# A hybrid decoder trunk on one core: GpSimd's weight sums start behind another tile

## The reference

```python
for l in range(DEPTH):                       # DEPTH = 2
    h = rms_norm(x, g_mix[l])
    z = h @ w_in[l]
    qa, ka, va, ga, ub, vb, qc, kc, vc, gates = split_cols(z)
    ya = silu(ga) * (rms_normalize(retention(rotary(qa), rotary(ka), va)) * ret_norm_g[l])
    yb = spatial_gating(gelu(ub), gelu(vb), ...)
    # 3 groups of dilated attention, combined by their softmax denominators
    yc = sum(softmax(lses)[g] * outs[g] for g in range(3))
    merged = sum(sigmoid(gates)[:, :, b] * (y[b] @ w_branch[l, b]) for b in range(3))
    x = x + merged @ w_o[l]
    h = rms_norm(x, g_ffn[l])
    gate, up = jnp.split(h @ w_gate_up[l], 2, axis=-1)
    x = x + (silu(gate) * up) @ w_down[l]
```

## Time and profile before

| | us |
|---|---|
| median of 3 runs | 1905.05 |
| profiled execution | 1904.88 |
| span of the profiled execution | 1903.1 |
| TensorE busy | 1889.8 |
| VectorE busy | 1241.8 |
| ScalarE busy | 850.4 |
| GpSimd busy | 96.9 |

### The profile page before, as it was taken

One profiled execution on the slowest core, in us unless ns is written; L12 is line 12 of the kernel. 1 busy time (PEld: TensorE's weight loads), 2 busy tenths in 40 slices (PEclk: granted clock), 3 DMA queues, 4 the chain that ended last, 5 costly groups with the idle time before them and its releaser, 6 DMA issues. The chain is left out here.

```text
span 1903.1 us, 26512 instructions
## 1 busy us (share of the span) xinstructions
PE 1889.8 (99%) x10600; PEld 1696.9 (89%) x10600; DVE 1241.8 (65%) x1617; ACT 850.4 (45%) x1190; POOL 96.9 (5%) x148
## 2 busy tenths in 40 slices
PE   8999999999999999999999999999999999999999
PEld 7888888888888899899888888888888888998998
DVE  7767746666566786377577677566665667863775
ACT  5544444444334464155335444444443344642554
POOL 0000001111111000000000000011111110000000
PEclk9999999999999999999999999999999999999999
DMA  5322347777787455366333222577777774653663
GB/s 203 94 75 71 86 114 206 193 195 197 200 213 208 125 177 174 100 191 197 122 100 95 68 78 80 143 191 194 207 199 197 210 195 128 189 160 104 201 211 123
DMA packets 85897, 295.68 MB, mean 155 GB/s; under 512 B 20368, under 2 KB 20624, under 8 KB 84624
## 3 DMA queue, kind: packets, MB, share of 16 engines
q1 hardware_dynamic: 73104, 218.49, 37.0%
q0 software_dynamic: 12672, 75.51, 17.5%
HBM read 291.79 MB, written 77.66 MB: 194 GB/s over the span
## 5 line engine op out<-in xcount | busy, mean ns | idle before, releaser
L1076 ACT ACTIVATE w_high<-raw 128x1024 fp32r<-128x1024 f32 x396 | 418.3, 1057 | 780.1 <-PE bank L851 651.0
L1284 DVE TENSOR_TENSOR w_low<-raw,w_high 128x1024 fp32r<-128x1024 f32 x396 | 483.0, 1222 | 142.8 <-ACT w_high L1076 136.1
L851 PE MATMUL bank<-h_high,w_high 128*128 128x512 f32 x1344 | 518.7, 386 | 9.0 <-DVE h_low L1289 8.2
L851 PE MATMUL bank<-h_low,w_high 128*128 128x512 f32 x1344 | 510.1, 380 | 0.0
L851 PE MATMUL bank<-h_high,w_low 128*128 128x512 f32 x1344 | 510.1, 380 | 0.0
L851 PEld LDWEIGHTS bank<-h_high,w_high 128*128 128x128 f32 x1344 | 254.7, 190 | 45.3 <-issue 8.2
L851 PEld LDWEIGHTS bank<-h_high,w_low 128*128 128x128 f32 x1344 | 254.5, 189 | 36.2
L851 PEld LDWEIGHTS bank<-h_low,w_high 128*128 128x128 f32 x1344 | 254.7, 189 | 35.1
L851 PE MATMUL bank<-in_high,w_high 128*128 128x512 f32 x672 | 255.4, 380 | 0.0
L851 PE MATMUL bank<-in_low,w_high 128*128 128x512 f32 x672 | 254.7, 379 | 0.0
L851 PE MATMUL bank<-in_high,w_low 128*128 128x512 f32 x672 | 254.7, 379 | 0.0
(11 more groups left out here) (166 smaller groups left out, 2451.7 us busy)
## 6 DMA issues: line engine op xcount, KB each, us to landing
raw<-weights SPq DMA_DIRECT2D x325, 512.0 KB, 4.2
weight_sums<-weights POOLq DMA_DIRECT2D x108, 512.0 KB, 6.5
raw<-weight_sums SPq DMA_DIRECT2D x72, 512.0 KB, 4.1
weight_sums<-weight_sums POOLq DMA_DIRECT2D x36, 512.0 KB, 4.0
turned<-rows SPq DMA_DIRECT2D x3, 768.0 KB, 7.4
xT<-x_t SPq DMA_DIRECT2D x8, 256.0 KB, 5.7
decay_sb<-decay SPq DMA_DIRECT2D x8, 256.0 KB, 4.0
out_t<-xT SPq DMA_DIRECT2D x8, 256.0 KB, 4.5
```

The lines of the kernel that those rows point to most:

```text
L851: return pe.matmul(o, w, m, start=start, stop=stop)
L1076: act.activation(w_high[:, PART_SLOT[s], :, :], raw[:, s % RAW_SLOTS, :, :], ACT.Copy).then_inc(part_high_w.sem, 1)
L1284: dve.tensor_tensor(w_low[:, PART_SLOT[s], :, :], raw[:, s % RAW_SLOTS, :, :], w_high[:, PART_SLOT[s], :, :], ALU.subtract).then_inc(part_ ...
```

## The change

One argument of one wait in GpSimd's program. The first DMA of the sums of a layer waited until VectorE had evacuated `("rq", 0)`; it now waits until VectorE has evacuated `("k", 3, 0)` of the same layer, 13 tiles earlier. No instruction comes or goes, and the instructions of all five engines stand in the same order as before.

```diff
@@ -706,7 +706,7 @@
             for layer in range(DEPTH):
-                pool.wait_ge(tile_stored.sem, tile_stored.at(layer * STRIDE, AT["rq", 0]))
+                pool.wait_ge(tile_stored.sem, tile_stored.at(layer * STRIDE, AT["k", HEADS - 1, 0]))
                 for n, u in enumerate(QUICK_UNITS):
                     first = AT["quick", u, 0]
```

## The result

| | kernel before | changed kernel |
|---|---|---|
| median of 8 runs, us | 1905.56 (1904.66 to 1906.71) | 1914.14 (1909.56 to 1918.63) |
| ratio, 95% interval | | 1.0045 (1.0036 to 1.0055) |
| profiled execution, us | 1904.88 | 1914.38 |
| its span, us | 1903.1 | 1912.6 |

The change costs 8.6 us at the median, and the runs now spread over 9 us where they spread over 2. The forecast was 1907.3 us with a range to 1912.0: too low, and the measured median lies outside.

A forecast was written before the change was run, and what follows sets the result against it. TensorE's queue was taken as the bound from end to end. Profiled 1904.88 us, no gain, plus 2.3 us of swap delay (1.3 and 1.0) gave 1907.2, plus 0.17 to the median: 1907.3 us, range 1904.5 to 1912.0.

The forecast's parts named there:

- What bounds, and that the end of the sums gains nothing: TensorE's queue bounds from end to end; sums ending sooner gain at most 0.21 us per layer.
- Weight loads of head 3 cost 0: Loads beside the early sums: closest has 11.7 us until its split on ScalarE, slowest landed after 8.6; cost 0.
- The bound of 8.6 us: Slowest landing of a weight load beside the sums in the old trace, taken as worst; still leaves 3 us.
- The swap is the transfer: Softmax maxima and sums, written to DRAM and read back reordered; four swaps, heads 2 and 3, now lie beside the sums.
- the margins of 2.28, 2.16, 0.62 and 2.16 us: How late swaps may be before TensorE waits: heads 2 and 3 of layer 0, then of layer 1; sum 7.22 us.
- most of all at 1154: Largest new TensorE wait foreseen at 1154 us, head 2 of layer 1, where the margin was 0.62 us.
- I take +1.9 per swap: Each swap's delay, two steps at the median weight load's +0.9; 1.3 us over margin at head 2, layer 1.
- The hit of the tail: One +2.6 us delay, as of a slow decay table, in one other swap: 1.4 us over margin, counted as 1.0.
- The rule of the Trainium skill that I had set against the change: A DMA's semaphore increment lands only after every earlier write of the same DMA engine, other queues included; not in the sum.
- Rival 2: Swap writes held behind the sums' transfers, about 3.5 us per swap; price 6.8 us, so 1911.9 us; chance 0.27.
- Then costs that wait in full: A change off TensorE costs nothing until TensorE waits for it, then the whole wait, as a full queue returns nothing.

The follow-up runs named there:

- The pair without the exchange: Early start of the changed kernel and late start of the kernel before, each without the pairs' exchange through DRAM: 1905.63 and 1905.50 us, both 1.0001 times the kernel before.
- the kernel with six additions: Kernel before, late start, plus six idle VectorE additions between the swap's landing and the shift step, heads 2 and 3: 1916.93 us, ratio 1.0059.

## Why the prediction was wrong, step by step

- **What bounds, and that the end of the sums gains nothing**: right. TensorE's queue is full, the old waits stand unchanged, and the kernels in which the early sums meet no swap are within 0.05% of the kernel before.
- **Weight loads of head 3 cost 0**: right. The pair without the exchange shows it, and in the changed kernel ScalarE waits for no weight load beside the attention of head 3. The bound of 8.6 us was too low, though: the load issued inside head 2's swap landed after 9.6 us in layer 0 and 10.6 in layer 1, and cost nothing because ScalarE had need of it later still.
- **The swap is the transfer, and the margins of 2.28, 2.16, 0.62 and 2.16 us**: right. Time was lost at the four places named, at three of them in a wait that the list shows; 1.4 us on VectorE cost nothing at the median, 4.2 us cost 11.8. The largest waits stood at head 3 (2.15 and 2.22 us), not "most of all at 1154" (1.09 us), and the 0.62 us were the margin of one slow swap and not of the place.
- **"I take +1.9 per swap"**: this step failed. A swap was 2.4 to 4.5 us later, 3.6 at the mean; that and the margins make the 7.1 us above, where the sum had 2.3. I had priced a pair transfer by the median weight load beside the sums, +0.95 for each of two steps (the rows give 4.5 - 3.6 = 0.9). A read took 1.0 to 2.7 us more, and a write of head 3 2.5 and 3.4 more. The median was the wrong number of that row: each swap had one step that was 2.4 to 3.4 us late, between the row's median, +0.9, and its worst, +5.0. The hit of the tail that the sum counted once, with 1.0 us, came at every swap. Why the median misled is in part argued: the loads of that row beside the sums (276 to 636 us) meet no swap. The trace of before had a nearer row that I did not look at: the weight load that SyncE issues right behind the pair writes of heads 2 and 3 landed after 5.9 to 6.8 us even without the sums, against 3.6 at the median elsewhere, so large transfers and pairs do disturb each other. The Trainium skill, "DMA: Bandwidth & Descriptors", section "Issuing engines are not separate DMA queues", says that DMAs of the sync and gpsimd engines interleave on the same 16 DMA engines; the reads agree, +3.4 us at head 3 of layer 0 even beside loads that write no DRAM. The rule of the Trainium skill that I had set against the change, on increments that wait for earlier writes of other queues, fits the writes of head 3, but so does plain sharing, and no run here separates the two.
- **Because the size was off, so were the chances.** Rival 2 took 3.5 us per swap and came to 6.8 us; measured 3.6 and 7.1. Its places and its price were right, and I gave it 0.27. Its mechanism, a write that is held, was half of it: of the 14.3 us by which the four swaps were late together, 6.3 are in the writes and 8.1 in the reads, and at head 2 the writes were hardly late at all (+0.6 and -0.3 us).
- **What no case had**: the halved clock. "Then costs that wait in full" let a wait cost itself and no more. Here a wait of 2 us can cost 1.7 more. The two runs with a mean clock of 1.000 are at 1909.6 and 1910.8 us; it is with the halved clock that the median came beyond rival 2's 1911.9.

## What to carry to other kernels

A short transfer that something waits for is priced by what may be in flight beside it when it is issued, not by the mean traffic; ask how late it may be, and put the margin against the tail. Background DMA work may be begun early if it pauses where such a transfer runs: one more wait on the background queue kept all 8.6 us away here. Where a queue is full, room is bought for the one consumer that has need of it; moving the same step for all heads cost 17 us.

## What the runs showed of the hardware that I had not expected

- TensorE's granted clock went from 1.00 to 0.50 (2.4 to 1.2 GHz) in or right behind some of its waits in front of the transposes and stayed for 3.4 us, in the changed kernel and equally with idle VectorE work as the only cause. It did so at 272.3 us, behind a wait of 2.15 us, but not behind 2.2 us at 1222; in the kernel with six additions behind both waits of layer 1 (2.2 and 2.1 us) and not behind those of 1.0 us in layer 0; with the start behind head 3's query tile at a wait of 3.0 us in layer 0 and not at 3.2 us in layer 1; with the later order for all heads behind waits of 0.8, 0.4 and 0.2 us in a row. What decides is open.
- The delay is mutual. The sums' first copies, issued beside head 2's swap, kept GpSimd from its next step for 9.8 us (194.04 to 203.79), where the same step took 5.4 us in the kernel before (from 275.32):

```profile
203.79 1.69 POOL L703 DMA_DIRECT2D weight_sums<-weights  x2 [8.60 <-DMA weight_sums<-weights]
```
```profile
280.72 1.69 POOL L703 DMA_DIRECT2D weight_sums<-weights  x2 [4.25 <-DMA weight_sums<-weights]
```

  These copies landed after 8.0 and 8.8 us, those of layer 1 after 7.7 and 8.3; in the kernel before no copy took more than 6.8. Plain loads to SBUF in the same place took 7.0 to 10.5 us, and 3.9 to 6.0 in the three rounds behind it in layer 0.
- The second write of 4 KB of pairs took 5.5 to 6.4 us to land at heads 2 and 3 even without the sums, with one weight load in flight beside it; a weight load of 512 KB lands after 3.6 us at the median.
